# Expert items of a mixture-of-experts layer taken by turns, a large one and a small one, in place of all small ones and then all large ones

## The reference, cut to what matters

```python
def _moe(h, w_router, b_router, w1, w3, w2):
    logits = (h @ w_router + b_router).astype(jnp.float32)
    top_l, top_e = lax.top_k(logits, MOE_TOPK)          # 2 of 8
    gates = jax.nn.softmax(top_l, axis=-1)
    ...
    def expert_group(args):
        xg, e = args
        return (jax.nn.silu(xg @ w1[e]) * (xg @ w3[e])) @ w2[e]
    ...
```

## Time and profile before

| | us |
|---|---|
| median of 3 runs | 1955.3 |
| lowest and highest | 1953.67, 1956.48 |
| the profiled execution | 1957.39 |
| its span, first to last instruction | 1955.6 |
| first unit of the experts cast, to the last one cast | 688.9 to 1914.1 |

### The profile page before, as it was taken

How to read it: one execution, slowest core, us unless ns; L and a number is a source line. 1 busy time by engine, 2 the same in 40 slices (tenths; PEclk the granted TensorE clock), 3 DMA queues, 4 the chain that set the end, 5 groups by cost and what they waited for, 6 DMA issues and landing times.

```text
span 1955.6 us, 26587 instructions
## 1 busy us (share of the span) xinstructions
PE 1812.1 (93%) x9702; PEld 1447.8 (74%) x9702; DVE 1506.4 (77%) x1568; ACT 1199.4 (61%) x1115; POOL 18.1 (1%) x73
## 2 busy tenths in 40 slices
PE   6988799999999789999999999999999999999997
PEld 3756489999887766776677677667777787787775
DVE  3677464555798589898998989899788787887884
ACT  2233254444456268787887878788676677676673
POOL 2000000000000000000000000000000000000000
PEclk7979799999899879999999999999999999999998
DMA  9578776555825159999999999999999798998970
GB/s 328 201 273 292 278 243 220 169 178 174 256 87 198 65 215 376 378 397 395 377 394 379 385 383 394 397 376 394 337 336 366 286 359 316 332 355 315 334 286 23
DMA packets 221527, 579.23 MB, mean 296 GB/s; under 512 B 10478, under 2 KB 73398, under 8 KB 221437
## 3 DMA queue, kind: packets, MB, share of 16 engines
q1 hardware_dynamic: 220429, 573.98, 79.9%
q0 software_dynamic: 1024, 4.25, 0.7%
HBM read 574.79 MB, written 4.35 MB: 296 GB/s over the span
## 4 chain that ended last, share of the span: by engine, by line
PE 67%; DVE 14%; issue 8%; ACT 7%; SPq 2%; DMA 1%; DVEq 1%; ACTq 0%; PEldq 0%
PE banks L961 18%; PE banks L491 14%; PE banks L949 13%; DVE w_lo L1894 9%; ACT w_hi L1273 4%; PE banks L772 3%; PE banks L919 3%; PE banks L792 2%; PE banks L905 1%; PE banks L865 1%; PE banks L547 1%; PE banks L883 1%; DMA ring<-in_ada_w_dram 1%; PE banks L567 1%; PE banks L530 1%
## 5 line engine op out<-in xcount | busy, mean ns | idle before, releaser
L1894 DVE TENSOR_TENSOR w_lo<-ring,w_hi 128x2048 fp32r<-128x2048 f32 x420 | 949.7, 2289 | 166.3 <-ACT w_hi L1273 166.3
L1273 ACT CAST w_hi<-ring 128x2048 fp32r<-128x2048 f32 x420 | 797.5, 1910 | 292.6 <-PE banks L961 177.7
L961 PE MATMUL banks<-w_hi,x_s 128*128 128x512 f32 x672 | 279.6, 416 | 43.5 <-DVE w_lo L1894 40.4
L949 PE MATMUL banks<-w_hi,g_buf 128*128 128x512 f32 x784 | 286.8, 406 | 9.7 <-DVE w_lo L1894 8.5
L961 PE MATMUL banks<-w_hi,x_m 128*128 128x512 f32 x896 | 289.8, 400 | 2.4 <-DVE w_lo L1894 2.4
L961 PE MATMUL banks<-w_lo,x_s 128*128 128x512 f32 x672 | 267.0, 397 | 0.0
L949 PE MATMUL banks<-w_lo,g_buf 128*128 128x512 f32 x560 | 221.2, 395 | 0.0
L1426 DVE TENSOR_TENSOR w_lo<-ring,w_hi 128x1024 fp32r<-128x1024 f32 x124 | 143.8, 1204 | 82.8 <-ACT w_hi L1094 81.8
L961 PEld LDWEIGHTS banks<-w_hi,x_s 128*128 128x128 f32 x672 | 127.1, 189 | 106.5 <-DVE w_lo L1894 76.8
L1094 ACT CAST w_hi<-ring 128x1024 fp32r<-128x1024 f32 x124 | 121.5, 1032 | 131.6 <-PE banks L491 55.0
L961 PEld LDWEIGHTS banks<-w_hi,x_m 128*128 128x128 f32 x896 | 169.1, 189 | 43.3 <-DVE w_lo L1894 2.9
(11 more groups left out here) (377 smaller groups left out, 2052.6 us busy)
## 6 DMA issues: line engine op xcount, KB each, us to landing
ring<-in_moe_w_dram SPq DMA_DIRECT2D x420, 1024.0 KB, 6.5
ring<-in_ada_w_dram SPq DMA_DIRECT2D x48, 1024.0 KB, 6.4
ring<-in_ffn_w_dram SPq DMA_DIRECT2D x30, 1024.0 KB, 5.2
ring<-in_attn_w_qkv_dram SPq DMA_DIRECT2D x12, 1024.0 KB, 12.5
ring<-in_conv_w_pw_dram SPq DMA_DIRECT2D x12, 1024.0 KB, 12.6
ring<-in_cache_k_dram SPq DMA_DIRECT2D x16, 512.0 KB, 7.7
ring<-in_cache_v_dram SPq DMA_DIRECT2D x16, 512.0 KB, 6.3
ring<-in_attn_w_o_dram SPq DMA_DIRECT2D x4, 1024.0 KB, 8.0
```

The costliest lines, as they stand in the source:

```text
L949: mm = pe.matmul(out_b[:, b, :], g, y, start=(p == 0 and t == 0 and i == 0), stop=(p == NCH - 1 and t == 2 * last + 1 and i == len(g_passe ...
L961: mm = pe.matmul(bk[:, b, :], x, y, start=(k == 0 and i == 0), stop=(k == KC - 1 and i == len(x_passes(k, hi, lo)) - 1), skip_group_check= ...
L1273: act.copy(w_unit(n)[0], ring[:, pos_of(n), :]).then_inc(ev("moe_hi_ready"), 1)
L1894: dve.tensor_tensor(lo, ring[:, pos_of(n), :], hi.bitcast(F32), ALU.subtract).then_inc(ev("moe_lo_ready"), 1)
```

## The change

One loop takes the place of two. In each turn `d` an engine runs the large item `d`, if there is one, and then the small item `d`, so that the order is: the unrolled small item, large, small, large, small, large, small, large, small, small. An item's number in the order of running no longer follows from the loop's counter. VectorE writes it into a new list, `turn_of`, in front of `moe_list_ready`, and each engine loads it in each turn. A small item now has two numbers: `q`, among the small ones, for the semaphores that only small items use, and `w`, among all. SyncE's loop, which held one body of 42 loads, now holds two. What an item computes and the steps within it are as before.

```diff
         def items(eng, first, small, large):
 
             first()
             eng.wait_ge(ev("moe_list_ready"), 1)
             n_small = eng.value_load(n_items[0:1, 0:1], min_val=0, max_val=MAX_SMALL)
-            with eng.Fori(0, MAX_SMALL) as d:
+            n_large = eng.value_load(n_items[0:1, 1:2], min_val=0, max_val=MAX_LARGE)
+            with eng.Fori(0, max(MAX_SMALL, MAX_LARGE)) as d:
+                with eng.If(n_large > d):
+                    large(d, eng.value_load(turn_of[0:1, 0, bass.ds(d, 1)], min_val=0, max_val=LIST) + 1)
+                eng.nop()
                 with eng.If(n_small > d):
-                    small(d)
-                eng.nop()
-            n_large = eng.value_load(n_items[0:1, 1:2], min_val=0, max_val=MAX_LARGE)
-            with eng.Fori(0, MAX_LARGE) as d:
-                with eng.If(n_large > d):
-                    large(d, eng.value_load(n_items[0:1, 0:1], min_val=0, max_val=MAX_SMALL))
+                    small(d + 1, eng.value_load(turn_of[0:1, 1, bass.ds(d, 1)], min_val=0, max_val=LIST) + 1)
                 eng.nop()
             return eng.value_load(n_items[0:1, 3:4], min_val=0, max_val=LIST)
...
-            def small(w, first=False):
+            def small(q, w, first=False):
                 for n in range(ES):
                     if n == 0:
-                        pe.wait_ge(ev("small_x_ready"), w + 1)
+                        pe.wait_ge(ev("small_x_ready"), q + 1)
...
-            last = items(pe, lambda: small(0, first=True), lambda d: small(d + 1),
-                         lambda d, n_small: large(d, n_small + d + 1))
+            last = items(pe, lambda: small(0, 0, first=True), small, large)
...
-            n_all, n_small = total[:, COLUMNS - 1:COLUMNS], total[:, NE - 1:NE]
+            n_all, n_small, n_large = total[:, COLUMNS - 1:COLUMNS], total[:, NE - 1:NE], dif[:, 0:1]
             step(dve.tensor_copy(n_items[:, 0:1], n_small))
             step(dve.tensor_tensor(n_items[:, 1:2], n_all, n_small, ALU.subtract))
+            step(dve.tensor_tensor(n_large, n_all, n_small, ALU.subtract))
...
             step(dve.tensor_copy(expert_of[:, :], list_f[:, 1, :]))
+            settle()
+            for k, count in ((0, n_small), (1, n_large)):
+                step(dve.tensor_scalar(list_f[:, k, :], iota_place[:, :], float(k), count, ALU.add, ALU.min))
+            settle()
+            for k in range(2):
+                step(dve.tensor_tensor(turn_of[:, k, :], list_f[:, k, :], iota_place[:, :], ALU.add))
             announce("moe_list_ready")
...
-            n_more = sp.value_load(n_items[0:1, 3:4], min_val=0, max_val=LIST)
-            with sp.Fori(0, LIST - 1) as i:
-                with sp.If(n_more > i):
-                    e = sp.value_load(expert_of[0:1, bass.ds(i, 1)], min_val=0, max_val=NE - 1)
-                    for s in range(ES):
-                        expert(e, i + 1, s)
-                sp.nop()
+            n_small = sp.value_load(n_items[0:1, 0:1], min_val=0, max_val=MAX_SMALL)
+            n_large = sp.value_load(n_items[0:1, 1:2], min_val=0, max_val=MAX_LARGE)
+            with sp.Fori(0, max(MAX_SMALL, MAX_LARGE)) as d:
+                for k, count, at in ((0, n_large, n_small + d), (1, n_small, d)):
+                    with sp.If(count > d):
+                        e = sp.value_load(expert_of[0:1, bass.ds(at, 1)], min_val=0, max_val=NE - 1)
+                        w = sp.value_load(turn_of[0:1, k, bass.ds(d, 1)], min_val=0, max_val=LIST) + 1
+                        for s in range(ES):
+                            expert(e, w, s)
+                    sp.nop()
```

More of the change, by code:

```diff
@@ L266, in build @@
         expert_of = sb("expert_of", [P, LIST], I32, at=moe)
+        turn_of = sb("turn_of", [P, 2, LIST], I32, at=moe)
         list_f = sb("list_f", [P, 2, LIST], at=moe)
@@ L1006, in small @@
                             pe.wait_ge(ev("moe_h1_kept"), NCH * (w + 1))
-                        rows_small(w + 1, (b,))
+                        rows_small(q + 1, (b,))
                     if n == TURN_AT[-1]:
@@ L1016, in small @@
                         pe.wait_ge(ev("moe_h3_kept"), NCH * (w + 1))
-                        cols_small(w + 1)
+                        cols_small(q + 1)
             def large(d, w):
@@ L1333, in small @@
                             if p == NCH - 1:
-                                keep_rows_small(w + 1)
+                                keep_rows_small(q + 1)
                             act.activation(g_cols[:, 0:256 * wide], t_b[:, 0, 0:256 * wide], ACT.Silu).then_inc(ev("moe_silu_ready"), 1)
                         if n == min(TURN_AT[p] + WBUF + 2, ES - 2):
-                            act.wait_ge(ev("moe_g_ready"), NCH * w + p + 1)
+                            act.wait_ge(ev("moe_g_ready"), NCH * q + p + 1)
                             g = g_buf[:, p % 2, 0:512 * wide].rearrange("p (t s n) -> p t s n", s=2, n=SMALL)
@@ L1340, in small @@
                                .then_inc(ev("moe_g_hi_ready"), 1)
-                keep_small(w + 1)
+                keep_small(q + 1)
             def large(d, w):
@@ L1363, in _ @@
             keep_small(0)
-            last = items(act, lambda: small(0, first=True), lambda d: small(d + 1),
-                         lambda d, n_small: large(d, n_small + d + 1))
+            last = items(act, lambda: small(0, 0, first=True), small, large)
             keep_out(last)
@@ L2014, in _, with select_small @@
             step(dve.tensor_copy(expert_of[:, :], list_f[:, 1, :]))
+            settle()
[4 more added lines that the diff above has]
+                step(dve.tensor_tensor(turn_of[:, k, :], list_f[:, k, :], iota_place[:, :], ALU.add))
             announce("moe_list_ready")
-            def select_small(w):
-                dve.wait_ge(ev("small_rows_filled"), 2 * w)
-                c = dve.value_load(column_of[0:1, bass.ds(w - 1, 1)], min_val=0, max_val=COLUMNS - 1)
+            def select_small(q):
+                dve.wait_ge(ev("small_rows_filled"), 2 * q)
+                c = dve.value_load(column_of[0:1, bass.ds(q - 1, 1)], min_val=0, max_val=COLUMNS - 1)
                 dve.tensor_copy(rank_c[:, :], rank_w[:, :, bass.ds(c, 1)].rearrange("p i o -> p (i o)")).then_inc(small_step, 1)
-                dve.wait_ge(small_step, 2 * w + 1)
+                dve.wait_ge(small_step, 2 * q + 1)
                 for i in range(3):
@@ L2025, in select_small, with large_column, select_large @@
                 last.then_inc(ev("small_sel_ready"), 1)
-            def select_large(d, w):
-                c = dve.value_load(column_of[0:1, bass.ds(w - 1, 1)], min_val=0, max_val=COLUMNS - 1)
+            def large_column(d):
+                return dve.value_load(column_of[0:1, bass.ds(first_large + d, 1)], min_val=0, max_val=COLUMNS - 1)
+            def select_large(d):
+                c = large_column(d)
                 dve.tensor_copy(rank_m[:, :], rank_w[:, :, bass.ds(c, 1)].rearrange("p i o -> p (i o)")).then_inc(ev("moe_large_step"), 1)
@@ L2064, in small @@
                             dve.wait_ge(ev("moe_gs_filled"), w)
-                            c = dve.value_load(column_of[0:1, bass.ds(w - 1, 1)], min_val=0, max_val=COLUMNS - 1)
+                            c = dve.value_load(column_of[0:1, bass.ds(q - 1, 1)], min_val=0, max_val=COLUMNS - 1)
                             dve.tensor_copy(gate_c[:, :], gate_w[:, :, bass.ds(c, 1)].rearrange("p i o -> p (i o)")).then_inc(small_step, 1)
-                            dve.wait_ge(small_step, 2 * w + 2)
+                            dve.wait_ge(small_step, 2 * q + 2)
                         gated(iota_twice, rank_c)
@@ L2072, in small @@
                         dve.wait_ge(ev("moe_gsel_ready"), w + 1)
-                        select_small(w + 1)
+                        select_small(q + 1)
                     for p, (j, wide) in enumerate(CHUNKS):
                         if n == min(TURN_AT[p] + WBUF + 1, ES - 2):
-                            dve.wait_ge(ev("moe_silu_ready"), NCH * w + p + 1)
+                            dve.wait_ge(ev("moe_silu_ready"), NCH * q + p + 1)
                             dve.wait_ge(ev("moe_gT_filled"), 2 * (NCH * w + p) + 2)
@@ L2102, in large @@
                         dve.wait_ge(ev("large_rows_filled"), 2 * d + 2)
-                        select_large(d + 1, w + 1)
+                        select_large(d + 1)
                     for p, (j, wide) in enumerate(CHUNKS):
@@ L2113, in large @@
                                               g_buf[:, p % 2, 0:512 * wide].bitcast(F32), ALU.subtract).then_inc(ev("moe_g_lo_ready"), 1)
-            select_large(0, dve.value_load(n_items[0:1, 0:1], min_val=0, max_val=MAX_SMALL) + 1)
-            last = items(dve, lambda: small(0, first=True), lambda d: small(d + 1),
-                         lambda d, n_small: large(d, n_small + d + 1))
+            first_large = dve.value_load(n_items[0:1, 0:1], min_val=0, max_val=MAX_SMALL)
+            select_large(0)
```

(1 more changed line is left out.)

## The result

The changed kernel takes 1996.0 us (median of 4 executions, 1991.0 to 1999.2) beside 1954.5 us for the kernel before on the same chip (median of 4, 1952.7 to 1956.5): a ratio of 1.0214, 95% interval 1.0199 to 1.0229. The forecast was 1971 with a range of 1954 to 1984, so the sign is right and the size is not: +41.5 in place of +16. The profiled execution took 1999.2 with a span of 1997.5.

The account below looks back on a forecast made before the run. It took small items as bound by the cast, lower, matmul ring and large ones by TensorE. Terms -3.5 + 0.0 + 0.65 + 0.3 + 11.7 + 4.0 + 2.9 = +16.0 us gave 1971, range 1954 to 1984.

Parts of the forecast that it names:

- What bounds the kernel: Expert part: small items bound by the cast, lower, matmul ring with three buffers, large ones by TensorE; earlier loads worth nothing.
- rival 4: Small items behind large ones: loads were the bound after all, so up to -34 us, 1921; chance 0.08.
- The seams: Where items meet: new small-to-large losses and large-to-small gains cancel to 0.0 us, with a doubt of 0.7.
- the registers: Loading the item's position each turn: mostly hidden, 0.3 us lost on TensorE behind the unrolled item.
- The old seam: Where all small items ended and large ones began: its idle time and slow clock vanish, a gain of 3.5 us.
- The list: VectorE's extra list operations before the expert items, on the path TensorE waits for: a loss of 0.65 us.
- Code: TensorE's jumps back over 144 KB may find code gone; 3.5 us a fetch, 11.7 plus 4.0 us in all.
- The three jumps: TensorE's jumps back that end on a large item: 3.9 us each with the slow clock, 11.7 in all.
- after one such turn only three places are needed, and they should stay: Empty turns at the kernel's end: argument that their code stays after one turn, against up to 31 us more.
- the end: Behind the last small item: three empty turns of two tests cost 1.8 us, 2.9 with a lowered clock.
- The fourth jump: TensorE's jump that tests past a large body to the last small item: one fetch, 4.0 us.
- Rival 3: Empty turns or other engines' jumps miss too: up to 31 us more at the end, 1978 to 2002; chance 0.17.

Follow-up runs that it names:

- the straight line: TensorE's turns written out without jumps, other engines looping as in the changed kernel, against which it differs only there: 1953.0 us, ratio to before 1.000.
- the counted loops: The kernel before, in its old order, with its two loops running only as many turns as the list has items: 1951.4 us, ratio 0.9988.

## Why the prediction was wrong, step by step

*What bounds the kernel* held. In the changed kernel too, from 934 to 1385, the casts wait for TensorE alone (78.0 and 40.8 us beside 46.2 and 38.4 in the earlier trace rows), and no landing appears; the straight line's 1.000 leaves nothing of rival 4's 34 us.

*The seams, the registers* held. A large item behind a small one was put at 132.11 + 0.74 + 0.1 + 0.3; from its predecessor's last unit to its own last the trace has 133.24 for L1 and 133.00 in the straight line, where no register is loaded, so the registers cost 0.24 for 0.3. A small item behind a large one was put at 113.89 less 0.64 and takes 113.27. The old seam's 3.5 shows in the counted loops, whose windows on both sides of it are 1.87 and 1.56 us shorter. *The list*, 0.65: the unrolled item takes 119.03 us from its first matmul to its last in place of 118.16, 0.87 more.

*Code* named the right mechanism and the right place, and **its price is the first step that failed**. 3.5 us a fetch was the middle of two shortest landings of stores and loads; the jumps took 4.6 to 7.4. With the measured jump the rest of the sum comes out: 5.04 less 1.2 hidden plus 1.6 of slow clock is 5.4, and S1 with L2 is 252.00 in place of the straight line's 246.31, so 5.7. The three jumps cost 18.1 (5.7, 6.9 and 5.6 by such pairs) for 11.7.

Busy DMA engines, by which I had chosen between the bounds, are not needed for the price: in the windows of the two long jumps among the empty turns the engines are at a share of 0.08 and 0.05, and these took 5.0 and 4.6. Packets do start sooner there, 0.6 to 0.9 us behind the jump, but two of them come for each jump, and the total is about the same.

```profile
1951.00:1956.00 5.00, 0.86 (x4) 0.38 (x2) 0.00 (x0) 1.01 (x1) 0.00 (x0) 0.80 0.08 10
1956.00:1961.00 5.00, 0.00 (x0) 0.00 (x0) 0.00 (x0) 0.00 (x0) 0.00 (x0) 0.50 0.05 10
```

**The second step that failed is "after one such turn only three places are needed, and they should stay".** The second empty turn missed twice, and the end costs 12.6 for 2.9 (the gap of 11.53 less 1.10, and a stretch behind it that is 2.2 longer at a lower clock). *The fourth jump*, put at 4.0 with one fetch, has up to three in a row in the profiled execution: the loop end 6.1, the skip 7.4, and 2.84 of idle time two matmuls into S5 while another packet comes. S4 is 12.1 longer than in the straight line and S5 4.2 without the gap behind it: 16.3. Where the skip is short, as in the second profile of the changed kernel, the whole is some 8 us shorter.

18.1 + 16.3 + 12.6 = 47.0 against the straight line, for terms that stood at 18.6: 28.4 too little, 12.3 at the fourth jump, 9.7 at the end and 6.4 at the other three. The profiled time missed by 25.8 (1999.2 less 1973.4); the 2.6 between lie mostly ahead of the loop, where the unrolled item ended 2.2 us earlier than before. Rival 3, which I gave 0.17, thus had the time (1978 to 2002), and its own sign, ten or more idle us behind the last item, is in the trace; the argument against it was the second step above. That its range held the time is in part luck: it put up to 31 us at the end, where 9.7 more than forecast were found, and the rest came from the other four jumps.

The Trainium skill, "Runtime: NRT & Kernel Launch", section "Instruction fetch mechanics", says that a taken branch out of what is held waits for a DMA, and that straight fetching is mostly hidden. The trace agrees with both: 4.6 to 7.4 us, and no gap in the straight line. Its 128 KiB for TensorE is no length that a loop may have: 124 KB missed at all four live jumps back and 103 KB at two of four, and there the measurement decides.

## What to carry to other kernels

Count the instructions of a loop body on each engine before bodies are merged into one loop: here a loop of 80 KB of TensorE's code jumped back free, one of 103 KB at two of four live turns, and those of 124 KB and more at none, at about 5 us a jump plus the clock that the gap costs. Empty turns and skipped branches jump too, and at the end of this kernel nothing covered their long jumps, so let loops count what there is. Price a fetch by a fetch: the rows of data transfers, loaded or not, gave a figure that was a third too low.

## What was not expected of the hardware

A long jump costs about the same on full DMA engines as on idle ones (5.0 and 5.0 us at a share of 1.02 and 0.08), but in other parts: at the changed kernel's loop ends of live turns 2.4 to 3.8 us until the last packet within the jump starts and 2.5 to 2.9 from there, at the end of the kernel 0.9 and 4.1. The same program misses at one jump in some executions and not in others (7.4 and 0.25 us at line 396), which moves its time by 8 us. With a hint 245 or 100 us ahead the live jumps stayed at 4.9 to 6.3 us; with one 10 us ahead two of four took 2.4 us, in the one execution profiled.
